# The opening of a two-block float32 kernel on one core: x and two weight units loaded in quarters on one queue, both units multiplied interleaved by quarter

## What is computed

```python
def rmsnorm(x, gain):
    xf = x.astype(jnp.float32)
    y = xf * lax.rsqrt(jnp.mean(xf * xf, axis=-1, keepdims=True) + EPS)
    return (y * gain.astype(jnp.float32)).astype(x.dtype)

def swiglu(x, w1, w3, w2):
    return (jax.nn.silu(x @ w1) * (x @ w3)) @ w2

def first_block(x, ...):
    ...
    h = h + 0.5 * swiglu(rmsnorm(h, ffn1_norm[l]), ffn1_w1[l], ffn1_w3[l], ffn1_w2[l])
    u = rmsnorm(h, mix_norm[l])
    ...            # token mixing (pooling and retention), a second swiglu, a norm

def reference(x, ...):
    x = first_block(x, ...)
    return second_block(x, ...)    # two attentions, a gated layer with a convolution
```

## Time and profile before

| | us |
|---|---|
| median of 3 runs | 834.4 (834.33 to 834.74) |
| the profiled execution | 834.21 |
| its span, first to last instruction | 832.4 |
| TensorE busy in it | 823.4 (99%) |
| VectorE busy | 625.1 (75%) |
| ScalarE busy | 439.5 (53%) |
| GpSimd busy | 89.8 (11%) |

### The profile page before, as it was taken

How to read it: one execution, slowest core, us unless ns; L and a number is a source line. 1 busy time by engine, 2 the same in 40 slices (tenths; PEclk the granted TensorE clock), 3 DMA queues, 4 the chain that set the end, 5 groups by cost and what they waited for, 6 DMA issues and landing times.

```text
span 832.4 us, 13214 instructions
## 1 busy us (share of the span) xinstructions
PE 823.4 (99%) x5041; PEld 711.0 (85%) x5041; DVE 625.1 (75%) x779; ACT 439.5 (53%) x559; POOL 89.8 (11%) x93
## 2 busy tenths in 40 slices
PE   9999999999999999999999999999999999999996
PEld 6888888888988888888888899878788988888895
DVE  5786766667977587667667779767874898998897
ACT  6555444546334554454444746566435556665664
POOL 0300000004450300000000317000003000000001
PEclk9999999999999999999999999999999999999999
DMA  8876566564844458756665594684545365466551
GB/s 260 304 239 213 188 194 204 170 201 151 254 153 151 152 185 259 246 194 201 198 205 152 130 243 125 175 259 150 177 157 181 118 204 200 151 206 216 183 176 52
DMA packets 115888, 157.69 MB, mean 189 GB/s; under 512 B 4445, under 2 KB 95997, under 8 KB 115725
## 3 DMA queue, kind: packets, MB, share of 16 engines
q1 hardware_dynamic: 113212, 150.56, 56.3%
q0 software_dynamic: 1392, 5.34, 1.9%
q10 hardware_dynamic: 1248, 1.32, 0.5%
HBM read 154.42 MB, written 1.07 MB: 187 GB/s over the span
## 4 chain that ended last, share of the span: by engine, by line
PE 96%; DVE 1%; DMA 1%; ACT 1%; issue 1%; POOL 0%; ACTq 0%; POOLq 0%; DVEq 0%
PE wk L1760 30%; PE acc L1882 20%; PE wk L1729 16%; PE wk L1768 16%; PE acc L1859 7%; PE acc L2173 1%; PE acc L1776 1%; PE wk L2209 1%; PE acc L1729 1%; DMA x<-in_x 1%; PE acc L2188 1%; PE wk L2246 0%; ACT w_hi L516 0%; PE acc L1895 0%; DVE w_lo L1061 0%
## 5 line engine op out<-in xcount | busy, mean ns | idle before, releaser
L1760 PE MATMUL wk<-xhl,w_hi 128*128 128x512 f32 x1104 | 268.9, 391 | 0.0
L1078 DVE TENSOR_TENSOR w_lo<-raw,w_hi 128x2048 fp32r<-128x2048 f32 x83 | 189.9, 2289 | 63.7 <-ACT w_hi L523 62.5
L1760 PEld LDWEIGHTS wk<-xhl,w_hi 128*128 128x128 f32 x1104 | 202.3, 188 | 39.3 <-issue 0.3
L523 ACT ACTIVATE w_hi<-raw 128x2048 fp32r<-128x2048 f32 x83 | 158.0, 1903 | 0.0
L1768 PEld LDWEIGHTS wk<-xhl,w_lo 128*128 128x128 f32 x1104 | 145.5, 191 | 8.0
L1768 PE MATMUL wk<-xhl,w_lo 128*128 128x256 f32 x1104 | 147.9, 282 | 0.0
L516 ACT ACTIVATE w_hi<-raw 128x2048 fp32r<-128x2048 f32 x51 | 97.0, 1911 | 53.7 <-PE wk L1729 28.4
L1061 DVE TENSOR_TENSOR w_lo<-raw,w_hi 128x2048 fp32r<-128x2048 f32 x44 | 101.3, 2302 | 24.9 <-ACT w_hi L516 24.7
L1882 PE MATMUL acc<-w_hi,hhl 128*128 128x512 f32 x480 | 119.4, 391 | 0.0
L1882 PEld LDWEIGHTS acc<-w_hi,hhl 128*128 128x128 f32 x480 | 88.2, 188 | 17.1
L1729 PE MATMUL wk<-xhl,w_hi 128*128 128x256 f32 x352 | 61.3, 286 | 0.0
(11 more groups left out here) (266 smaller groups left out, 977.9 us busy)
## 6 DMA issues: line engine op xcount, KB each, us to landing
raw<-in_ffn_w SPq DMA_DIRECT2D x64, 1024.0 KB, 5.3
raw<-in_w_in SPq DMA_DIRECT2D x24, 1024.0 KB, 7.2
raw<-in_w_ffn_in SPq DMA_DIRECT2D x22, 1024.0 KB, 5.0
raw<-in_w_ffn_out SPq DMA_DIRECT2D x11, 1024.0 KB, 4.9
raw<-in_w_out SPq DMA_DIRECT2D x8, 1024.0 KB, 4.9
arena<-bias_scratch POOLq DMA_DIRECT2D x4, 512.0 KB, 6.2
raw<-in_w_in SPq DMA_DIRECT2D x4, 512.0 KB, 7.0
raw<-in_cmp_w_k SPq DMA_DIRECT2D x2, 1024.0 KB, 5.5
```

The lines of the kernel that those rows point to most:

```text
L523: nc.scalar.activation(w_hi[:, s], raw[:, s], ACT.Copy).then_inc(hi_done, 1)
L1078: nc.vector.tensor_tensor(w_lo[:, s], raw[:, s], w_hi[:, s].bitcast(F32), ALU.subtract) \
L1760: mm = nc.tensor.matmul(bank, wh[:, c, cols], xhl[:, c].rearrange("p n t -> p (n t)"), start=c == 0, stop=False, skip_group_check=True)
```

## The change

The change works on the opening in five ways. Units 0 and 1 are both loaded in quarters.

1. **Loads.** x's quarters move from ScalarE's queue to SP's, and SP issues them between the quarters of units 0 and 1: x, 0, 1, x, 0, 1, x, 0, x, 0, 1, 1. The identity moves from SP's queue to ScalarE's, ahead of the gain. The seventeen small transfers move from ahead of unit 3 to behind it, ahead of unit 4.
2. **TensorE.** `opening_unit` and `second_unit` become `opening_units`: products of both units interleaved by quarter, four banks in use. Warming products are 5 and 2 where they were 8, 2 and 2.
3. **ScalarE and VectorE** follow that order. The high part of x's chunk 1 is made by VectorE, and the first chunk waits for its own two transposes instead of four. One of the four squares moves ahead of the copy of unit 0.
4. **Vectors and root.** TensorE turns the vectors and spreads the root behind unit 2, which is now an ordinary `col_unit`. ScalarE makes unit 3's high part ahead of `vectors`.
5. Semaphores are merged (identity and gain; vectors and convolution rows; sinks and gate weights).

```diff
-                sp.dma_start(sink[:], a["attn_sinks_2"][0].partition_broadcast(P)).then_inc(sink_in, 16)
-                sp.dma_start(wg_raw, w_cols(a["w_in_2"][0])[:, :, 2048:2072]).then_inc(wg_in, 16)
+                sp.dma_start(sink[:], a["attn_sinks_2"][0].partition_broadcast(P)).then_inc(late_in, 16)
+                sp.dma_start(wg_raw, w_cols(a["w_in_2"][0])[:, :, 2048:2072]).then_inc(late_in, 16)
+            def opening_loads(c1, c3):
+                def x_piece(p):
+                    cols = slice(p * UC, (p + 1) * UC)
+                    sp.dma_start(x[:, :, cols], a["x"][0].rearrange("(t p) n -> p t n", p=P)[:, :, cols]) \
+                        .then_inc(x_in[p], 16)
+                def w_piece(s, src, p, got):
+                    sp.dma_start(k_n(raw[:, s], DC)[:, 2 * p:2 * p + 2], src[:, 2 * p:2 * p + 2, 0:UC]) \
+                        .then_inc(raw_in[s] if p == 3 else got[p], 16)
+                for p in range(2):
+                    x_piece(p)
+                    w_piece(0, c1, p, first_in)
+                    w_piece(1, c3, p, second_in)
+                for p in (2, 3):
+                    x_piece(p)
+                    w_piece(0, c1, p, first_in)
+                for p in (2, 3):
+                    w_piece(1, c3, p, second_in)
...
                 unit(base + 2, c1[:, :, UC:2 * UC], DC)
+                unit(base + 3, c3[:, :, UC:2 * UC], DC)
                 if base == U_FFN1:
                     small_loads()
-                unit(base + 3, c3[:, :, UC:2 * UC], DC)
                 unit(base + 4, r2[:, 0:2, :], 2)
...
-            sp.dma_start(cst[:, 0:P], a["c_small"][:, 0:P]).then_inc(ident_in, 16)
...
-            act.dma_start(vec_rows[V_FFN1:V_FFN1 + DC, :], rows8(a["ffn1_norm"][0])).then_inc(gain_in, 16)
-            for p in range(4):
-                cols = slice(p * UC, (p + 1) * UC)
-                act.dma_start(x[:, :, cols], a["x"][0].rearrange("(t p) n -> p t n", p=P)[:, :, cols]) \
-                    .then_inc(x_in[p], 16)
+            act.dma_start(cst[:, 0:P], a["c_small"][:, 0:P]).then_inc(front_in, 16)
+            act.dma_start(vec_rows[V_FFN1:V_FFN1 + DC, :], rows8(a["ffn1_norm"][0])).then_inc(front_in, 16)
...
                 if f == 0:
-                    for b in range(BANKS):
+                    for b in range(1, BANKS):
                         square(0, b)
                     b_part(0, base + 2)
+                    hi(base + 3)
                     vectors()
-                    hi(base + 3)
                     tanh(0)
                     hi(base + 4)
...
+            dve.wait_ge(gain_ready, 1)
+            dve.wait_ge(turned, 1)
+            nc.vector.tensor_scalar(xh[:, 1], chunk_at(0, 1), vec[:, V_FFN1 + 1:V_FFN1 + 2], None, ALU.mult) \
+                .then_inc(xh_ready, 1)
+            x_lo(0, 0, V_FFN1)
+            x_lo(1, 0, V_FFN1)
+            lo_piece(0, 0)
+            lo_piece(1, 0)
...
+                    col_unit(s2, 0, i * 3 + base, whole).then_inc(unit_done, 1)
                     if spreads:
-                        spread_unit(s2, 0, i * 3 + base).then_inc(unit_done, 1)
-                    else:
-                        col_unit(s2, 0, i * 3 + base, whole).then_inc(unit_done, 1)
+                        turn_vectors()
+                        spread(n, acc[:, 0])
```

More of the change, by code:

```diff
@@ L626, in vectors @@
                     .then_inc(vec_ready, 1)
-            for p in range(4):
-                hi_piece(p)
-                if p == 0:
-                    act.wait_ge(gain_ready, 1)
-                x_hi(2 * p, 0, V_FFN1)
-                x_hi(2 * p + 1, 0, V_FFN1)
-            hi_half(0)
-            hi_half(1)
+            act.wait_ge(gain_ready, 1)
+            x_hi(0, 0, V_FFN1)
+            hi_piece(0, 0)
+            hi_piece(1, 0)
+            x_hi(2, 0, V_FFN1)
+            x_hi(3, 0, V_FFN1)
+            hi_piece(0, 1)
+            hi_piece(1, 1)
+            x_hi(4, 0, V_FFN1)
+            x_hi(5, 0, V_FFN1)
+            hi_piece(0, 2)
+            hi_piece(0, 3)
+            x_hi(6, 0, V_FFN1)
+            x_hi(7, 0, V_FFN1)
+            hi_piece(1, 2)
+            hi_piece(1, 3)
+            square(0, 0)
             ffn(0, U_FFN1)
@@ L1791, in keep_warm, with opening_units, high, low @@
                     nc.tensor.matmul(wk[:, 3], zeros[:, 0:P], zeros[:], start=True, stop=True)
-            def opening_unit():
-                keep_warm(8)
-                pe.wait_ge(ident_in, 16)
-                pe.wait_ge(gain_in, 16)
+            def opening_units():
+                def high(slot, p):
+                    if p == 3:
+                        pe.wait_ge(hi_done, slot + 1)
+                    else:
+                        pe.wait_ge((hi_first, hi_second)[slot], p + 1)
+                    for c in (2 * p, 2 * p + 1):
+                        if slot == 0:
+                            pe.wait_ge(xl_ready, c + 1)
+                        for t in range(2):
+                            split_high(slot, t, wk[:, 2 * slot + t], (c,))
+                def low(slot, p):
+                    if p == 3:
+                        pe.wait_ge(lo_done, slot + 1)
+                    else:
+                        pe.wait_ge((lo_first, lo_second)[slot], p + 1)
+                    for c in (2 * p, 2 * p + 1):
+                        for t in range(2):
+                            mm = split_low(slot, t, wk[:, 2 * slot + t], (c,))
+                    return mm
+                def turned_x(p):
+                    pe.wait_ge(x_in[p], 16)
+                    turn_pair(0, p)
+                keep_warm(5)
+                pe.wait_ge(front_in, 16 * 2)
@@ L1816, in opening_unit @@
-                return mm
+                high(0, 0)
+                turned_x(1)
+                pe.wait_ge(gain_ready, 1)
+                high(1, 0)
+                low(0, 0)
+                low(1, 0)
+                high(0, 1)
+                turned_x(2)
+                high(1, 1)
+                low(0, 1)
+                turned_x(3)
+                low(1, 1)
+                high(0, 2)
+                low(0, 2)
+                high(0, 3)
+                low(0, 3).then_inc(unit_done, 1)
@@ L1818, in first_unit @@
+                high(1, 2)
+                high(1, 3)
+                low(1, 2)
+                low(1, 3).then_inc(unit_done, 1)
             def first_unit(slot, n, parted):
```

111 lines of the change are left out of this document (42 added, 69 removed).

## The result

| | before | after |
|---|---|---|
| median | 834.52 us, 20 runs (834.19 to 835.9) | 835.84 us, 20 runs (833.6 to 838.26) |
| profiled execution | 834.21 | 835.38 |
| its span | 832.4 | 833.6 |

The ratio after / before is 1.0018, 95% interval [1.0011, 1.0026]. The forecast was 833.1 with a range of 832.5 to 834.3. The change made the kernel slower by 1.3 us, within the 0.2% that the prediction counted as "same", but outside its range. One run further down, 859.12 of e1, had a granted clock of 0.911 where all others had 0.996 to 0.999, and no ratio holds it.

What follows compares the result with a forecast made beforehand. TensorE was taken as the bound (96% of the chain), up to its wait at unit 5: a start at 36.4 instead of 37.66 gains 1.3, giving 832.9, or 833.1 as median; range 832.5 to 834.3.

Steps and rivals of the forecast that it cites:

- Part 1: Opening, first real TensorE product: starts at 5.7 us instead of 7.92, with x's first quarter landed at 4.0.
- Part 2: Units 0 and 1: 0.3 waiting for x's second quarter at 6.9, then dense; end 18.76 instead of 20.21, 1.45 earlier.
- the row taken for the level: First real products: two warming products taking 0.59 before were read as the higher clock level there; no cost counted.
- The sum: Unit 5's start moves from 37.66 to 36.4, so 1.3 us gained and a time of 833.1.
- the clock: Rival, opening: thinner warming delays the clock rise; a rise at 8 costs 0.7, at 9.2 the whole gain: 834.4; chance 0.10.
- Part 3: Vectors' and root's transposes on TensorE behind unit 2: 0.1 gained (0 to 0.2); unit 3 could start at 24.9.
- Part 4: ScalarE and VectorE chain from unit 3's low part, at 23.4, to unit 5: 12.79, so unit 5 at 36.2.
- Part 5: Small loads between units 3 and 4: unit 4's load lands 5.6 after issue, costing 0.2: unit 5 at 36.4.
- unit 4 late: Rival, unit 4's load: lands 6.6 after issue, at 28.5; unit 5 at 37.4, gain 0.3, time 834.1; chance 0.18.
- the other side: Rival, unit 4's load: lands 8.5 after issue, at 30.4; unit 5 at 39.3, 1.6 later than before: 836.0; chance 0.05.

Runs made afterwards that it cites:

- e1: The changed kernel with 7 and 4 warming products instead of 5 and 2; median 834.1 us, ratio to the kernel before 1.0002.
- e12: The kernel before with 8, 4 and 2 warming products instead of 8, 2 and 2; median 834.45 us, ratio to the kernel before 1.0.
- e4: The kernel before with only the vectors' transposes and root's spread behind unit 2, and unit 3's high part ahead of the vectors' copies; median 834.7 us, ratio 1.0.
- e3: The changed kernel with x's four quarters on ScalarE's queue behind identity and gain; median 839.43 us, ratio to the kernel before 1.0061.
- e11: The changed kernel with 7 and 5 warming products instead of 5 and 2; median 834.03 us, ratio to the kernel before 0.9997.
- e6: The changed kernel with 14 and 3 warming products instead of 5 and 2; median 836.03 us, ratio to the kernel before 1.0016.
- e5: The changed kernel with the gain issued ahead of the identity on ScalarE's queue and 5, 1 and 4 warming products; median 837.67 us, ratio to before 1.0033.
- e8: The changed kernel with the identity first on SP's queue, the gain alone on ScalarE's, and 5, 2 and 4 warming products; median 835.11 us, ratio to before 1.0009.

## Why the prediction was wrong, point by point

**Part 1, the first product: 6.90, not 5.7.** Three terms failed. x's first quarter came at 4.3 for 4.0, and TensorE has to turn the gain first, which landed at 4.26: the transposes started at 4.58. The prediction had no term for the gain, although the change moved it from first to second on its queue: 0.6 for both. The two pairs of transposes took 1.06 at the lower level for 0.51: 0.5. And handing over took 0.1 more, over several steps, than assumed. In e1 the transposes took 0.60, but its two extra warming products let them start only at 4.81, and the first product came at 6.67.

**Part 2.** x's second quarter was predicted for 6.9, and no wait for it appears in the timeline of after or e1; the predicted 0.3 of waiting was swallowed by the later first product. The feeders hold, as predicted: no wait above 0.1 stands in the timeline of TensorE between the first product and the end of units 0 and 1. But these end at 20.98, not 18.76: 1.2 from the first product and 1.0 from the stretch behind it. In e1 that stretch, from first product to the end of units 0 and 1, is 12.52; the prediction had 13.06, after has 14.08. So the lower level cost 1.56 there, and the prediction had 0.54 in hand.

**The failed step is the row taken for the level.** "By the row the higher level is there when the first product starts, and the sum stands" rested on two warming products that took 0.59 in a kernel with eight and two ahead of them, hardly a gap between. The sum put nothing on the level of the first real work. Measured, it is worth 1.8: unit 5 starts at 38.74 in after and at 36.93 in e1. The rival **the clock** had the mechanism and part of the price: it put 1.3 on a rise at 9.2, and in the trace the rise comes at about 10.2, with 1.59 lost between 6.90 and 11.02 (the same groups take 4.12 in after and, 6.67 to 9.20, 2.53 in e1). Its chance of 0.10 was too low for a change that takes five of twelve warming products out and lets two waits in between. Its price stopped at the whole gain, where its own formula, for a rise at 10.2, gives (10.2 - 6)/2 - 0.3 = 1.8 and so a loss of 0.5. The rest of the miss is that the gain was itself too large: 0.73 in the profiled execution of e1, for 1.3. What the Trainium skill says in "TensorE: Matmul & The Clock Gate", Part 1, that the same kernel meets a different number of products at the lower clock from run to run, was cited and then outweighed by one trace. The runs here do not contradict it: one profiled execution of before could show the level of that execution only, and after spreads over 4.7 us. That the seven runs from 837.38 up are those in which the level rose latest is argued, not shown; none of them has a trace, and e12 shows that a late landing can lengthen a run too. Nor is it known why they stand apart from the other thirteen.

**Part 3.** The vectors are turned at 26.56 right behind unit 2, without a wait. Its worth, 0 to 0.2, is too small for e4 to show.

**Part 4** holds where it matters: from the low part of unit 3 to unit 5, 38.74 - 25.94 = 12.80 for the predicted 12.79, and 0.47 of waiting for 0.3. It was a chain and not TensorE's work that set unit 5, and what is lost ahead of it arrives there undiminished, which e3 shows at 3.6 us. One reading in it was wrong. It put the 1.40 that VectorE idled in before down to the vectors' copies on ScalarE. These were done at 21.40, and ScalarE then stood for unit 3's load, which SP had issued behind the small ones:

```profile
22.92 1.91 ACT L516 ACTIVATE w_hi<-raw 128x2048 fp32r<-128x2048 f32 x1 [1.52 <-DMA raw<-in_ffn_w]
```

So the start of the chain in before, 24.87, hung on a landing, and TensorE's own work (the row unit in the chain, 32.30 + 5.47) ended at 37.77, 0.1 behind the 37.66 at which that chain let unit 5's weights load. By these rows (it was not run) an earlier first product alone would have gained 0.1 there, and it took an earlier unit 3 as well, which the change brought.

**Part 5.** The small loads take 17.62 to 24.27, 6.7 as predicted, 2.4 later than predicted, as all that hangs on units 0 and 1. Unit 4's load goes out at 24.31, and its high part starts at 30.04, 0.1 after the tanh (29.31 + 0.63): the load has landed within 5.7, for 5.6. The predicted 0.2 was not paid in after, where the low parts of units 3 and 4 start 6.06 apart as before; it was in e11, and 0.3 in e6. The rivals "unit 4 late" and "the other side" did not occur. The time came out near the latter's 836.0 by another mechanism, which is chance.

**The sum.** With the clock cured the forecast gain of 1.3 is not reached: in e1 unit 5 starts 0.73 earlier than before, the profiled execution is 0.62 shorter, the median 0.35 lower, and the ratio, 1.0002, is that of no gain at all. In the profiled execution the difference to the prediction is part 1: 0.97 late, of which the shorter way from there to unit 5 (30.26 for 30.7) gives 0.4 back.

## What to carry to other kernels

When an opening is made shorter, its warming products are part of what is moved. Look at what TensorE does from its first instruction to the first real product: in after, five and two warming products with a hole of 0.51 ahead of the gain cost more than everything that the new order gained, and in e1 seven and four without that hole cost nothing. The wait of 0.42 ahead of the first real product stood in both. e1 changed both counts at once, so which of the two matters more is not shown. Give the clock a term of its own in the sum, with the row of the first products at each level as its two prices, and run it against a version in which only the gaps are filled. Of what an engine turns first, the smallest transfer counts as much as the largest: a 4 KB piece that is second on its queue landed at 4.26, about when the 256 KB beside it did. And before a wait is put down to the order of an engine's program, read what released the engine ahead of it.

## What the hardware showed that was not expected

- The page's granted clock prints 1.00 for windows of 2 to 8 us in which products of 512 columns took 0.43 each. For the first microseconds the length of a known product is the better reading.
- Two kernels with the same number of warming products behind the transposes (four, in e1 and e5) start real work at different levels. Ahead of the transposes e1 has seven without a hole, e5 five, a hole of 1.20 and one. Waits of 0.20 to 0.63 with denser warming around them (e1, e6, e8, e11) went with the higher level at the first product. Each is one execution.
- A transfer of 4 KB took 3.04 from its issue to landing behind 64 KB on ScalarE's queue, and 4.04 from GpSimd, where it was alone. The 256 KB first in SP's queue took 3.6, and the 64 KB of the identity, first there in the kernel before, 1.9. In these first microseconds size did not tell the landing.
- The same load of unit 3, behind the same small transfers, took 6.46 and 7.43 in e4 and e12, and the chain passed it on to unit 5 in both.
